# Turning five of nine input row tiles by VectorE blocks and a DRAM round trip instead of by TensorE

## The chip, the cores and the metric

The kernel runs on one core of one Trainium2 chip. The metric is the device time of one execution in microseconds (us), lower is better. The profile is of one execution; its times are in us unless marked ns.

## What is computed

One step of a decoder layer for a prompt of 1024 rows and 64 rows of new tokens (8 sequences of 8). Every row is normalised, and one wide projection feeds two attention branches and the merge gates:

```python
h = rms_norm(x, norm_g).astype(x.dtype)          # x / rms(x), times norm_g per column
z = jnp.einsum('bsd,de->bse', h, w_in)           # D_MODEL 1024, all projections side by side
...
qb = rms_norm(qb.reshape(b, s, B_HEADS, 2, HEAD_DIM), q_norm_b)
```

After that come the attention of both branches, their projections, the gates and the output projection. The change touches only the normalised input `h` and the way in which it comes to lie transposed, with the 1024 columns of the model on the partitions.

## The kernel before

The program is written by hand, one instruction stream per engine, with counted semaphores between them; each engine does its stream in the order in which it is written. Rows come in nine tiles: 0 to 7 are the prompt's (128 rows each, `NT` is 8), tile 8 is the sample's 64 rows. Weights come in blocks of 1024 x 512 (`u` is the block's number). A block is multiplied with all nine row tiles before the next one, eight chunks `k` of 128 columns each, three matmuls a chunk (`products`, L2074 to L2076), since every fp32 operand is split in a high and a low part. A row tile of a block is thus 24 matmuls. In this document "row r" of the first block is row tile r, and its "start" is its first matmul.

The first block, u = 0, is the q projection of branch B. While it runs, the row tiles are still being prepared, each in a relay over five engines:

- SyncE loads `xt` (`load_x`, L733), two buffers.
- ScalarE squares it with a running sum (`input_square`, L1292); GpSimd turns the sum into 1/rms (`input_rstd`, L1051 and L1052).
- VectorE scales the rows into `xn` (`rows_scale`, L1594).
- TensorE turns `xn` in two halves of four 128 x 128 transposes into bank 4 to 7 of PSUM (`turn_x`, L2030); of tiles 2 and up into bank 7 alone, so that a half waits until VectorE has read the one before.
- VectorE multiplies by the norm's gain on the way out of PSUM into `hn` (`input_gain`, L1603).
- ScalarE rounds to the high part (`input_hi`, L1268), GpSimd subtracts for the low part (`input_lo`, L1058), both into `hT`. TensorE's row waits for the low part (`h_lo`).

At row i of the block the engines have this work in their streams: TensorE turns tile i + 2 between its chunks; ScalarE and GpSimd do hi and lo of tile i + 3, and square and 1/rms of tile i + 4; VectorE does the gain of tile i + 3 and the scaling of tile i + 4. Between them stands what row i itself yields: a square of its result (ScalarE, L1335), the sum per head (VectorE, L1658), 1/rms (GpSimd), the scaled result `zn` (VectorE, L1673), its turning in 32 x 32 blocks (VectorE, L1679) and its store by SyncE (`store_blocks`, L768), and the splitting of one chunk of the next block's weights into high (ScalarE, L1281) and low part (VectorE, L1587). SyncE's own stream at row i (`block_io`) is `load_x(i+3)`, a weight chunk of the next block, `store_blocks` of row i - 1.

A DMA that moves 32 x 32 blocks between DRAM and the chip does so in pieces of 128 bytes. The kernel has such loads already: after the q and k projections it loads `qT` and `kT` from the blocks stored before (`load_turned`, L781).

## Time and profile before

| | |
|---|---|
| median of 3 runs | 1658.04 us |
| lowest, highest | 1654.12, 1663.19 us |
| the profiled execution | 1655.49 us, its span 1653.5 us |
| TensorE busy | 1597.9 us, 97% of the span |
| VectorE, GpSimd, ScalarE busy | 46%, 42%, 34% |
| granted TensorE clock | 0.994 of full speed over the span |

The span runs from the first to the last instruction of the engines; the profiled execution's own time is 2 us above it. The page has the share of each engine, the chain of work that ended last and the costliest groups; the trace behind it gives each instruction's start and length, what its engine waited for ahead of it, and the DMA queues. A duration in a timeline is that of one instruction or, where the row says xN, of N in a row.

### The profile page before, as it was taken

To read this page: it belongs to the slowest core of one execution; us is meant where nothing else is said; L and a number is where in the kernel's file an instruction comes from. 1 tells how busy PE (TensorE), PEld (TensorE's weight loads), DVE (VectorE), ACT (ScalarE), POOL (GpSimd) and SP (SyncE) were. 2 spreads that over 40 slices of the span, in tenths; PEclk is the share of its full clock that TensorE was granted. 3 is DMA by queue.
4 is the path that set the end of the run, shared out by engine and by line. 5 is a ranking of instruction groups with operands and counts; after the bars stand their busy time and mean duration, and the time that the engine had idled before them with its cause. 6 is when DMAs were issued, how large, how long until landed. Compare 5 with 4: busy or idle time off the path is not lost.

```text
span 1653.5 us, 37307 instructions
## 1 busy us (share of the span) xinstructions
PE 1597.9 (97%) x14616; PEld 1373.3 (83%) x14616; DVE 757.4 (46%) x1852; ACT 564.2 (34%) x1341; POOL 697.7 (42%) x958
## 2 busy tenths in 40 slices
PE   6999999999999999999999989999999899999999
PEld 5787677878899999999999877778787788888787
DVE  6632577332473332733326545344454433588411
ACT  5321477121362222712126233333343334411300
POOL 5676340466543666446666112222121121665500
PEclk9999999999999999999999999999999999999999
DMA  5358897337982369933797899889988977865593
GB/s 165 111 148 189 270 305 233 101 85 153 262 283 86 90 158 248 321 108 96 172 260 250 304 303 323 280 306 316 325 292 297 332 251 238 290 197 171 196 332 100
DMA packets 351487, 369.84 MB, mean 224 GB/s; under 512 B 164113, under 2 KB 208274, under 8 KB 351314
## 3 DMA queue, kind: packets, MB, share of 16 engines
q1 hardware_dynamic: 306354, 308.55, 61.9%
q10 hardware_dynamic: 44960, 58.92, 10.7%
q8 instruction: 117, 1.92, 0.5%
q14 instruction: 56, 0.46, 0.1%
HBM read 310.83 MB, written 143.85 MB: 275 GB/s over the span
## 4 chain that ended last, share of the span: by engine, by line
PE 84%; DVE 4%; DMA 3%; POOL 3%; issue 2%; ACT 2%; SPq 1%; ACTq 1%; POOLq 0%; DVEq 0%
PE ps L2074 13%; PE ps L2075 13%; PE ps L2076 13%; PE ps L2127 5%; PE ps L2128 5%; PE ps L2129 5%; PE ps L2230 4%; PE ps L2287 4%; PE ps L2176 4%; PE ps L2250 3%; PE ps L2348 3%; PE ps L2237 2%; PE ps L2331 2%; DMA v_in<-in_cache_a_kv 2%; PE ps L2197 2%
## 5 line engine op out<-in xcount | busy, mean ns | idle before, releaser
L1071 POOL TENSOR_TENSOR w_lo<-raw,w_hi 128x512 fp32r<-128x512 f32 x140 | 181.3, 1299 | 400.8 <-ACT w_hi L1281 399.9
L2074 PE MATMUL ps<-w_hi,hT 128*128 128x512 f32 x824 | 333.0, 404 | 2.1 <-POOL hT L1058 1.0
L2075 PE MATMUL ps<-w_lo,hT 128*128 128x512 f32 x824 | 330.1, 401 | 0.0
L2076 PE MATMUL ps<-w_hi,hT 128*128 128x512 f32 x824 | 330.1, 401 | 0.0
L2127 PE MATMUL ps<-w_hi,hT 128*128 128x256 f32 x768 | 225.3, 293 | 4.3 <-issue 3.9
L2074 PEld LDWEIGHTS ps<-w_hi,hT 128*128 128x128 f32 x824 | 206.2, 250 | 22.8 <-issue 1.4
L2076 PEld LDWEIGHTS ps<-w_hi,hT 128*128 128x128 f32 x824 | 206.2, 250 | 20.4
L2075 PEld LDWEIGHTS ps<-w_lo,hT 128*128 128x128 f32 x824 | 206.4, 250 | 19.4
L2129 PE MATMUL ps<-w_hi,hT 128*128 128x256 f32 x768 | 216.8, 282 | 1.0 <-issue 1.0
L2128 PE MATMUL ps<-w_lo,hT 128*128 128x256 f32 x768 | 217.4, 283 | 0.0
L1125 POOL TENSOR_SCALAR qz<-qT,qcol 64x128 f32<-64x128 f32 x256 | 156.0, 609 | 108.6 <-PE ps L2176 54.8
L1281 ACT ACTIVATE w_hi<-raw 128x512 fp32r<-128x512 f32 x158 | 98.7, 628 | 279.2 <-DMA raw<-in_w_in 237.0
L2127 PEld LDWEIGHTS ps<-w_hi,hT 128*128 128x128 f32 x768 | 147.3, 192 | 12.1 <-issue 11.5
L2128 PEld LDWEIGHTS ps<-w_lo,hT 128*128 128x128 f32 x768 | 147.6, 192 | 1.8 <-issue 1.8
L2129 PEld LDWEIGHTS ps<-w_hi,hT 128*128 128x128 f32 x768 | 147.2, 192 | 0.0
L1801 DVE STREAM_TRANSPOSE k_in<-k_in 128x512 f32<-128x512 f32 x224 | 138.5, 678 | 3.9 <-DMA k_in<-in_cache_a_kv 2.6
L1052 POOL TENSOR_TENSOR rs<-ss,half_pow 128x8 f32<-128x8 f32 (+3 forms) x81 | 127.0, 1568 | 6.7
L1673 DVE TENSOR_TENSOR zn<-ps,rs 128x512 f32<-128x512 f32 (+1 forms) x72 | 49.7, 691 | 145.5 <-POOL rs L1052 145.5
L1391 ACT ACTIVATE sA<-sA,st_sum 128x128 f32<-128x128 f32 (+1 forms) x192 | 86.1, 449 | 58.3 <-DVE st_sum L1767 52.4
L1335 ACT ACTIVATE ps<-ps 128x512 f32<-128x512 f32 (+1 forms) x72 | 41.8, 580 | 182.1 <-PE ps L2076 173.6
L1658 DVE TENSOR_REDUCE ss<-ps 128x8 f32<-128x512 f32 (+1 forms) x72 | 49.7, 690 | 117.0 <-ACT ps L1335 116.9
L2230 PE MATMUL ps<-kT,qz 128*128 128x128 f32 (+1 forms) x384 | 100.4, 348 | 1.0 <-issue 0.8
(229 smaller groups left out, 2758.7 us busy)
## 6 DMA issues: line engine op xcount, KB each, us to landing
out<-in_cache_a_kv SPq DMA_DIRECT2D x32, 2040.0 KB, 13.5
k_in<-in_cache_b_kv SPq DMA_DIRECT2D x128, 256.0 KB, 4.4
v_in<-in_cache_b_kv SPq DMA_DIRECT2D x128, 256.0 KB, 6.3
raw<-in_w_in SPq DMA_DIRECT2D x104, 256.0 KB, 3.4
k_in<-in_cache_a_kv SPq DMA_DIRECT2D x104, 256.0 KB, 8.1
v_in<-in_cache_a_kv ACTq DMA_DIRECT2D x96, 256.0 KB, 6.4
out<-in_cache_a_kv SPq DMA_DIRECT2D x8, 2016.0 KB, 10.3
raw<-in_w_in ACTq DMA_DIRECT2D x40, 256.0 KB, 6.8
```

The costliest lines, as they stand in the source:

```text
L1052: return pool.tensor_tensor(out, in_, half_pow[0:r, 0:heads], ALU.pow)
L1071: pool.tensor_tensor(lo, raw_of(q), hi.bitcast(F32), ALU.subtract).then_inc(lo_done, 1)
L1125: return pool.tensor_scalar(qz[rows, half, cols], qT[rows, c * SEQ + i * P:c * SEQ + (i + 1) * P], qcol[rows, (0 if G else 1):(0 if G else ...
L1281: act.activation(weights(q)[0], raw_of(q), ACT.Copy).then_inc(hi_done, 1)
L1801: dve.transpose(k_in[:, gg % NKS, j, :], k_in[:, gg % NKS, j, :]).then_inc(s_kt, 1)
L2074: pe.matmul(z, hi, wh, start=first, stop=False)
L2075: pe.matmul(z, hi, wl, start=False, stop=False)
L2076: return pe.matmul(z, lo, wh, start=False, stop=last)
L2127: pe.matmul(part, hi, wh, start=k == 0, stop=False)
L2128: pe.matmul(part, hi, wl, start=False, stop=False)
L2129: ins = pe.matmul(part, lo, wh, start=False, stop=k == KC - 1)
L2230: pe.matmul(bank(s % 4)[:, 0:W], qz[:, hh, i * P:(i + 1) * P], kT[:, k0:k0 + W], start=True, stop=True).then_inc(aq, 1)
```

## The change

Row tiles 3 to 7 (`BY_BLOCKS`) no longer go over TensorE and PSUM. VectorE multiplies the rows by 1/rms and by the gain in one instruction (the gain lies as `grow`, one copy of `norm_g` on each partition, loaded once), and turns the result in place in 32 x 32 blocks, 128 x 1024 at once. SyncE stores it to a DRAM scratch with four DMAs of 32 partitions each, in such an order that the scratch holds the tile transposed (`store_x`), waits until they have landed, and loads it back as `xT` (`load_xT`). ScalarE and GpSimd take high and low part from `xT` instead of `hn`. Tiles 0, 1, 2 and 8 go the old way.

With it the order changes: hi and lo of a turned tile t stand at row t - 2 of ScalarE's and GpSimd's streams, both halves together and at the row's end, where they stood at row t - 3 with other work between the halves. SyncE issues `load_x(i+5)` at row i behind `store_blocks`, where it issued `load_x(i+3)` ahead of it, and the weight chunks one row earlier. Semaphores used later in the program are used for the new waits too, and their later counts are raised.

```diff
@@ -212,6 +212,9 @@
...
         lamv = place("lamv", [P, 4, HD], at=at)
+        xT = place("xT", [P, 2, KC, P], at=at)
+        grow = place("grow", [P, D_MODEL], at=at)
+        assert at[0] <= work
@@ -316,6 +319,7 @@
...
         blocks_scr = [[dram(f"blocks_scr{g}{kind}", [SEQ, CW]) for kind in "qk"] for g in range(4)]
+        x_scr = [dram(f"x_scr{i}", [D_MODEL, P]) for i in range(TILES)]
@@ -406,6 +413,18 @@
...
             return turn_out[m % 2], 16 * sum(x % 18 % 9 < NT for x in range(m % 2, m + 1, 2))
+        def x_stored(i):
+            return st_in, 64 * (i - BY_BLOCKS[0] + 1)
+        def x_loaded(i):
+            return (kt_in if i % 2 else qt_in), 16 * len(range(BY_BLOCKS[0] + (i + BY_BLOCKS[0]) % 2, i + 1, 2))
+        def x_turns(i):
+            return i if i < BY_BLOCKS[0] else BY_BLOCKS[0]
@@ -573,6 +592,10 @@
...
             return half, (NT, *range(NT))[at_] if half else at_
+        def hi_lo_at(i):
+            return [t for t in (i + 2, i + 3) if (t in BY_BLOCKS) == (t == i + 2) and BY_BLOCKS[0] <= t <= NT]
@@ -746,6 +769,7 @@
...
             load_x(2)
+            sp.dma_start(grow[:, :], norm_g[0].partition_broadcast(P)).then_inc(s_const, 16)
@@ -754,6 +778,20 @@
...
                                  vec[0].rearrange("(d o) -> d o", o=1)).then_inc(s_const, 16)
+            load_x(4)
+            def store_x(i):
+                sp.wait_ge(ew_exp, i - BY_BLOCKS[0] + 1)
+                for a in range(0, P, 32):
+                    sp.dma_start(x_scr[i][:, a:a + 32].rearrange("(b r) c -> r b c", r=32),
+                                 xn[a:a + 32, i % 2, :].rearrange("p (b c) -> p b c", c=32)).then_inc(x_stored(i)[0], 16)
+            def load_xT(i):
+                sp.wait_ge(*x_stored(i))
+                if i - 2 in BY_BLOCKS:
+                    sp.wait_ge(h_lo, 2 * i - 2)
+                sp.dma_start(xT[:, i % 2, :, :], x_scr[i].rearrange("(k p) c -> p k c", p=P)).then_inc(x_loaded(i)[0], 16)
@@ -783,14 +821,18 @@
...
                 for at_, i in row_tiles(kind):
-                    if u == 0 and 4 <= i + 3 < TILES:
-                        load_x(i + 3)
...
                         constants()
-                    if at_ < KC:
-                        load_chunk(u + 1, at_)
+                    for k in ((0, 1) if at_ == 0 else (at_ + 1,)) if u == 0 else (at_,):
+                        if k < KC:
+                            load_chunk(u + 1, k)
...
                         store_blocks(G, kind, i - 1)
+                    if u == 0 and i + 5 < TILES:
+                        load_x(i + 5)
+                    if u == 0 and i + 3 in BY_BLOCKS:
+                        store_x(i + 3)
+                        load_xT(i + 3)
@@ -1056,6 +1098,7 @@
...
                     pool.tensor_tensor(hT_part(1, half, i),
+                                       xT[:, i % 2, 4 * half:4 * half + 4, :] if i in BY_BLOCKS else
@@ -1099,9 +1142,10 @@
...
                     if u == 0:
-                        input_lo(i + 3, 0)
                         input_rstd(i + 4)
-                        input_lo(i + 3, 1)
+                        for t in hi_lo_at(i):
+                            input_lo(t, 0)
+                            input_lo(t, 1)
@@ -1264,10 +1308,13 @@
...
                 if i < TILES:
-                    act.wait_ge(h_hn, 2 * i + half + 1)
-                    act.activation(hT_part(0, half, i),
-                                   hn[:, half, :].rearrange("p (k r) -> p k r", k=4)[:, :, 0:nrows(i)],
-                                   ACT.Copy).then_inc(h_hi, 1)
+                    if i in BY_BLOCKS:
+                        act.wait_ge(*x_loaded(i))
+                        part = xT[:, i % 2, 4 * half:4 * half + 4, :]
+                    else:
+                        act.wait_ge(h_hn, 2 * x_turns(i) + half + 1)
+                        part = hn[:, half, :].rearrange("p (k r) -> p k r", k=4)[:, :, 0:nrows(i)]
+                    act.activation(hT_part(0, half, i), part, ACT.Copy).then_inc(h_hi, 1)
@@ -1287,7 +1334,7 @@
...
                     if i >= 2:
-                        act.wait_ge(h_t, 2 * i - 2)
+                        act.wait_ge(*(x_stored(i - 2) if i - 2 in BY_BLOCKS else (h_t, 2 * i - 2)))
@@ -1335,8 +1382,6 @@
...
                         move(G)
-                    if u == 0:
-                        input_hi(i + 3, 0)
@@ -1344,7 +1389,9 @@
...
                         input_square(i + 4)
-                        input_hi(i + 3, 1)
+                        for t in hi_lo_at(i):
+                            input_hi(t, 0)
+                            input_hi(t, 1)
@@ -1591,12 +1638,19 @@
...
                     dve.wait_ge(h_rs, i + 1)
+                    if i in BY_BLOCKS:
+                        dve.wait_ge(s_const, 80)
+                        dve.scalar_tensor_tensor(out=xn[:, i % 2, :], in0=xt[:, i % 2, :], scalar=rs_x[:, i % 2, 0:1],
+                                                 in1=grow[:, :], op0=ALU.mult, op1=ALU.mult).then_inc(h_xn, 1)
+                        dve.wait_ge(h_xn, i + 1)
+                        dve.transpose(xn[:, i % 2, :], xn[:, i % 2, :]).then_inc(ew_exp, 1)
+                        return
...
             def input_gain(i, half):
-                if i < TILES:
-                    r, j = nrows(i), 2 * i + half
+                if i < TILES and i not in BY_BLOCKS:
+                    r, j = nrows(i), 2 * x_turns(i) + half
@@ -2021,7 +2075,7 @@
...
             def turn_x(i, half):
-                r, j = nrows(i), 2 * i + half
+                r, j = nrows(i), 2 * x_turns(i) + half
@@ -2089,7 +2143,7 @@
...
                         ins = products(bank(z_bank(n)), hi, lo, hTs[:, k, :], first_chunk[u] + k, i, k == 0, k == K - 1)
-                        if u == 0 and k in ((1, 5) if i else (4, 7)) and i + 2 < TILES:
+                        if u == 0 and k in ((1, 5) if i else (4, 7)) and i + 2 < TILES and i + 2 not in BY_BLOCKS:
```

VectorE, end of the preparation and rows 0 and 1 of the first block, before (`w_lo_72` is the first block's weight buffer, `w_lo_74` the second's, which the rows' weight splits fill):

```order
L1594 TENSOR_SCALAR xn<-xt,rs_x 128x1024 [waits h_rs]
L1603 TENSOR_TENSOR hn<-ps,gcol 128x512 [waits h_lo,h_t] x2
L1658 TENSOR_REDUCE ss<-ps 128x8 [waits sq_ready]
L1603 TENSOR_TENSOR hn<-ps,gcol 128x512 [waits h_lo,h_t]
L1673 TENSOR_TENSOR zn<-ps,rs 128x512 [waits rs_ready]
L1679 STREAM_TRANSPOSE zn<-zn 128x512 [waits zn_ready]
L1587 TENSOR_TENSOR w_lo_74<-raw,w_hi_73 128x512 [waits hi_done]
L1603 TENSOR_TENSOR hn<-ps,gcol 128x512 [waits h_lo,h_t]
L1594 TENSOR_SCALAR xn<-xt,rs_x 128x1024 [waits h_rs]
L1691 TENSOR_SCALAR qcol<-qcol 128x2 [waits s_const]
L1658 TENSOR_REDUCE ss<-ps 128x8 [waits sq_ready]
```

The same place of the changed kernel:

```order
L1643 SCALAR_TENSOR_TENSOR xn<-xt,rs_x,grow 128x1024 [waits s_const,h_rs]
L1646 STREAM_TRANSPOSE xn<-xn 128x1024 [waits h_xn]
L1657 TENSOR_TENSOR hn<-ps,gcol 128x512 [waits h_lo,h_t] x2
L1712 TENSOR_REDUCE ss<-ps 128x8 [waits sq_ready]
L1727 TENSOR_TENSOR zn<-ps,rs 128x512 [waits rs_ready]
L1733 STREAM_TRANSPOSE zn<-zn 128x512 [waits zn_ready]
L1634 TENSOR_TENSOR w_lo_74<-raw,w_hi_73 128x512 [waits hi_done]
L1643 SCALAR_TENSOR_TENSOR xn<-xt,rs_x,grow 128x1024 [waits s_const,h_rs]
L1646 STREAM_TRANSPOSE xn<-xn 128x1024 [waits h_xn]
L1745 TENSOR_SCALAR qcol<-qcol 128x2 [waits s_const]
L1712 TENSOR_REDUCE ss<-ps 128x8 [waits sq_ready]
```

The gains of the turned tiles are gone from the rows; weighting and turning stand where the scaling stood, ahead of the next row's sum and, for tile 3, ahead of the gains of tile 2.

GpSimd, rows 1 and 2 of the first block, in the changed kernel:

```order
L1093 TENSOR_SCALAR ss<-ss 128x8 [waits ss_ready]
L1094 TENSOR_TENSOR rs<-ss,half_pow 128x8 [waits pool_step]
L1093 TENSOR_SCALAR ss_x<-ss_x 128x1 [waits h_ss]
L1094 TENSOR_TENSOR rs_x<-ss_x,half_pow 128x1 [waits pool_step]
L1100 TENSOR_TENSOR hT_50<-xT,hT_49 128x4x128 [waits h_hi] x2
L1093 TENSOR_SCALAR ss<-ss 128x8 [waits ss_ready]
L1094 TENSOR_TENSOR rs<-ss,half_pow 128x8 [waits pool_step]
```

The two low halves of a tile stand together behind both 1/rms; before, the first stood between them.

SyncE, the stretch of rows 0 and 1, in the changed kernel:

```order
L756 DMA xt<-in_x_prompt 128x1024 [waits h_xn]
L787 DMA x_scr<-xn 32x32x32 [waits ew_exp]
L787 DMA x_scr<-xn 32x32x32 x3
L794 DMA xT<-x_scr 128x8x128 [waits st_in]
L763 DMA raw<-in_w_in 128x512 [waits lo_done]
L806 DMA blocks_scr0q<-zn 128x512 [waits blocks_turned]
L756 DMA xt<-in_x_prompt 128x1024 [waits h_xn]
```

Before, a row had three DMAs here (`raw`, `blocks_scr0q`, `xt`); now SyncE also issues the four stores, and stands at the load until they have landed, with the next weight chunk, the store of the row's blocks and the next `xt` behind it.

## Rows read from the trace of the kernel before

**Rows 1.** The page, chain that ended last: shares of the span by engine.

```profile
PE 84%; DVE 4%; DMA 3%; POOL 3%; issue 2%; ACT 2%; SPq 1%; ACTq 1%; POOLq 0%; DVEq 0%
```

**Rows 2.** Stretches: length, busy us of PE, PEld, DVE, ACT, POOL; clock, DMA share, GB/s.

```profile
26.54:60.91 34.37, 33.35 (x161) 25.98 (x159) 23.91 (x36) 16.75 (x32) 27.47 (x31) 1.00 0.40 124
506.00:508.00 2.00, 2.00 (x10) 2.00 (x10) 0.00 (x0) 0.00 (x0) 0.00 (x0) 1.00 0.19 17
```

**Rows 3.** Timeline, TensorE, first block: start us, us, instruction, idle before and releaser.

```profile
24.68 0.63 PE L2030 MATMUL ps<-ident,xn 128*128 128x128 f32 x4 [0.74 <-DVE hn L1603]
25.06 0.48 PE L2074 MATMUL ps<-w_hi,hT 128*128 128x512 f32 x1
26.54 0.60 PE L2030 MATMUL ps<-ident,xn 128*128 128x128 f32 x4
...
40.79 0.66 PE L2030 MATMUL ps<-ident,xn 128*128 128x128 f32 x4 [0.45 <-DVE xn L1594]
...
66.19 0.40 PE L2074 MATMUL ps<-w_hi,hT 128*128 128x512 f32 x1
...
71.79 0.40 PE L2072 MATMUL ps<-w_hi,hTs 128*128 128x512 f32 x1
```

**Rows 4.** Timeline, VectorE, row tiles 0 and 1 of the first block.

```profile
23.18 0.75 DVE L1594 TENSOR_SCALAR xn<-xt,rs_x 128x1024 f32<-128x1024 f32 x1 [0.45 <-POOL rs_x L1052]
23.85 0.68 DVE L1603 TENSOR_TENSOR hn<-ps,gcol 128x512 f32<-128x512 f32 x1
...
27.22 0.69 DVE L1658 TENSOR_REDUCE ss<-ps 128x8 f32<-128x512 f32 x1 [1.18 <-ACT ps L1335]
...
33.52 1.27 DVE L1691 TENSOR_SCALAR qcol<-qcol 128x2 f32<-128x2 f32 x1
34.70 0.68 DVE L1658 TENSOR_REDUCE ss<-ps 128x8 f32<-128x512 f32 x1
...
37.43 0.69 DVE L1673 TENSOR_TENSOR zn<-ps,rs 128x512 f32<-128x512 f32 x1 [1.46 <-POOL rs L1052]
...
38.79 0.68 DVE L1587 TENSOR_TENSOR w_lo<-raw,w_hi 128x512 fp32r<-128x512 f32 x1
```

**Rows 5.** Timeline, GpSimd, the same stretch.

```profile
33.48 1.28 POOL L1058 TENSOR_TENSOR hT<-hn,hT 128x512 fp32r<-128x512 f32 x1 [0.66 <-ACT hT L1268]
35.46 0.20 POOL L1051 TENSOR_SCALAR ss<-ss 128x8 f32<-128x8 f32 x1 [0.70 <-DVE ss L1658]
35.75 1.65 POOL L1052 TENSOR_TENSOR rs<-ss,half_pow 128x8 f32<-128x8 f32 x1
...
38.74 0.19 POOL L1051 TENSOR_SCALAR ss_x<-ss_x 128x1 f32<-128x1 f32 x1
39.01 0.86 POOL L1052 TENSOR_TENSOR rs_x<-ss_x,half_pow 128x1 f32<-128x1 f32 x1
```

**Rows 6.** Groups by line and shape, VectorE: count, busy us, mean ns, idle before.

```profile
L1801 DVE STREAM_TRANSPOSE k_in<-k_in 128x512 f32<-128x512 f32 x224 | 138.5, 678 | 3.9 <-DMA k_in<-in_cache_a_kv 2.6 <-DMA k_in<-in_cache_b_kv 1.0
L1728 DVE SCALAR_TENSOR_TENSOR sB<-sB,wB 128x1024 f32<-128x1024 f32 x4 | 5.1, 1287 | 0.1
L1915 DVE STREAM_TRANSPOSE k_new<-k_new 128x128 f32<-128x128 f32 x8 | 2.5, 311 | 0.1
```

**Rows 7.** Timeline, SyncE issuing: kT loads (1024 pieces each), statistics stores (128 pieces each).

```profile
400.85 4.26 SPq L781 DMA_DIRECT2D kT<-blocks_scr1k  x4
...
406.08 4.13 SPq L781 DMA_DIRECT2D kT<-blocks_scr1k  x4
...
503.44 4.61 SPq L875 DMA_DIRECT2D st_scr<-st  x8
```

**Rows 8.** DMA issues of three stretches: count, KB each, median us to landing.

```profile
kT<-blocks_scr1k SPq DMA_DIRECT2D x16, 128.0 KB, 4.7
...
xt<-in_x_prompt SPq DMA_DIRECT2D x8, 512.0 KB, 3.8
...
st_scr<-st SPq DMA_DIRECT2D x8, 8.0 KB, 1.5
```

More of the change, by code:

```diff
@@ L392, in build_step @@
         N_CONST = 16 * 8
+        BY_BLOCKS = range(3, NT)
+        X_TURNED, X_STORED, X_LOADED = len(BY_BLOCKS), 64 * len(BY_BLOCKS), (32, 48)
         N_COPIES = len(COPY_PARTS) * DEC_B
@@ L1137, in pad_first @@
                 pool.wait_ge(setup, 1)
-                pool.wait_ge(qt_in, 256 * (G + 1))
+                pool.wait_ge(qt_in, X_LOADED[0] + 256 * (G + 1))
                 for i in range(NT) if G else TILE_ORDER:
@@ L1518, in _ @@
                 if gg == N_GROUPS + 3:
-                    act.wait_ge(ew_exp, 1)
+                    act.wait_ge(ew_exp, X_TURNED + 1)
                     act.activation(ew[:, :, :, :], ew[:, :, :, :], ACT.Exp).then_inc(ew_exp, 1)
@@ L1689, in block_ @@
                         if i == 0:
-                            dve.wait_ge(s_const, 64)
+                            dve.wait_ge(s_const, 80)
                             dve.tensor_scalar(qcol[:, :], qcol[:, :], -(HD ** -0.5), None, ALU.mult)\
@@ L1818, in group_weights @@
             def group_weights():
-                dve.wait_ge(st_in, 48)
+                dve.wait_ge(st_in, X_STORED + 48)
                 def nm(g):
@@ L1830, in group_shares @@
             def group_shares():
-                dve.wait_ge(ew_exp, 2)
+                dve.wait_ge(ew_exp, X_TURNED + 2)
                 for g in range(3):
@@ L1921, in _ @@
                         dve.wait_ge(o_out, stored(3))
-                        dve.wait_ge(s_const, 64 + 16 * 6)
+                        dve.wait_ge(s_const, 80 + 16 * 6)
                     for i in range(4):
@@ L2260, in _ @@
                 pe.wait_ge(t_moved, G + 1)
-                pe.wait_ge(kt_in, 256 * (G + 1))
+                pe.wait_ge(kt_in, X_LOADED[1] + 256 * (G + 1))
                 attention_a(G) if G else attention_b()
```

## The prediction

> **What bounds the kernel now.** I read the page first, then the stretch of the first block, then each engine's timeline in it. TensorE is busy for 97% of the span (the table), and 84% of the span is its work on the chain that ended last [rows 1]: time taken from or put into its stream moves the end, nearly one for one, and after the first block its stream is unchanged. So the question is when TensorE leaves the first block. Tile 3's first turn starts at 26.54, tile 8's at 60.91 (the stretch in [rows 2]); between them lie five rows of 24 matmuls and the ten turning groups of tiles 3 to 7. TensorE is busy 33.35 of these 34.37 us, though VectorE only 23.91 and GpSimd 27.47. Row 7 has no turns and takes 71.79 - 66.19 = 5.60 us [rows 3]; five such rows are 28.0. The rest, 34.37 - 28.0 = 6.4 us, is what turning costs: ten groups at some 0.54, and waits for `xn` of 0.45 at the first half of tile 5 [rows 3] (one like it at tile 4). Every other engine has room only because a row takes 6.7 us.
>
> **What the change removes.** Forty transposes in ten groups, with their waits: at most 6.4 us, if each row's low part is there in time. The ten gains on VectorE (0.68 each, as that of tile 2 [rows 4]) go too; they are simply missing from the lists below.
>
> **What it adds on VectorE.** Weighting reads two SBUF operands of 128 x 1024; the same instruction and shape takes 1.29 us elsewhere [rows 6]. The bounds are 0.75, the plain scaling it replaces [rows 4], and 1.29 plus the low half of 1.28 that it may have to wait for (see the low halves, below). I take 1.29. The turning of 128 x 1024 has no row: 128 columns take 0.31 and 512 take 0.68 [rows 6], so on the line through them 1.17; twice 0.68 is the upper bound, 1.36. I take 1.2. The pair is 2.5 us where 0.75 stood.
>
> **The preparation.** The pair of tile 3 stands ahead of the gains of tile 2: the first of them starts at 23.85, right behind the scaling of 23.18 [rows 4], and will start 1.8 us later. TensorE's second turn of tile 2 waits for it (the idle 0.74 at 24.68), and row 1 follows that turn, at 25.06 [rows 3]. So row 1 starts at 26.9 and the sum of row 0 on VectorE, at 27.22 before, at 29.0. This 1.8 is on the path and nothing covers it.
>
> **One row of VectorE's stream.** From a row's sum to its `zn` 2.7 us (34.70 to 37.43; GpSimd's part of it is the wait for 35.46, then 35.75 plus 1.65 [rows 4, 5]), from `zn` over its own turning to the weight split 1.4 (37.43 to 38.79), the split 0.65, weighting 1.3, turning 1.2: 7.2 us, against 5.6 that TensorE needs. Before, the same cycle had two gains (one within the wait for GpSimd) and the scaling, some 6.2, and fitted the row of 6.7. For tile 4: 29.0 + 7.2 = 36.2, plus the small scaling of `qcol`, so row 1's sum starts at 36.5 though its matmuls are done at 32.5.
>
> **How the two low halves fit in.** `qcol` is 128 x 2 and yet took 1.27 us at 33.52, until 34.8, which is when GpSimd's low half of 33.48 ended (1.28 long) [rows 4, 5]. A VectorE scaling in SBUF stood still until GpSimd's subtraction was over. I assume the same for the weight split and the weighting, which read two operands from SBUF, and none for the turning. In the changed order a row on GpSimd, counted from the sum's start, is: 1/rms of the row done at 2.7, that of the next tile (38.74 to 39.87, 1.1 [rows 5]) at 3.8, first low half to 5.1. The split, due at 4.1, waits until 5.1 and ends at 5.75; the second low half goes to 7.05; the weighting to 8.3, the turning to 9.5. So the cycle is **9.5 us**, not 7.2.
>
> The Trainium skill, SBUF — State Buffer, "Who interferes with whom", says that a VectorE instruction with two SBUF inputs and a GpSimd instruction that reads SBUF exclude each other for their whole length. By that rule the weighting waits too, which the trace shows only for the plain scaling; without it, the sum would be that of the first rival.
>
> **When rows start.** Row t needs its first low half, at 5.1 after the sum of row t - 2. Row 3: 36.5 + 5.1 = 41.6 (before: 40.79 less the wait of 0.45 and six matmuls of 0.23, 38.9). Rows 4, 5, 6 follow at 9.5 each: 51.1, 60.6, 70.1. Tile 7 is turned at 36.5 + 3 x 9.5 = 65.0.
>
> **The round trip.** Four stores in pieces of 128 bytes. The nearest rows are loads of such pieces: four kT loads are issued in 4.26 us, and the next four follow 5.2 later with a weight chunk between [rows 7], so 4.3 us of DMA for four. A last landing takes between 1.5 (stores of 64-byte pieces) and 4.7 (kT loads that queue) [rows 8]; the last store is issued some 3.2 behind the first, so all have landed after 4.7 to 7.9. I take 6.2. `xT` is as large as an `xt` load, 3.8 us [rows 8], 3.9 with the wait. On SyncE the next weight chunk, `store_blocks` and `xt` queue behind this wait; with four issues of some 0.4 a tile costs it 6.2 + 1.7 = 7.9, under 9.5, so tiles 4 to 6 are there in time (tile 5 turned at 46.0, back at 56.2, its high part wanted around 59). Tile 3 has 11 us more. For tile 7 nothing is ahead: 65.0 + 6.2 + 3.9 = 75.1, high part 0.65 as before, low half 1.3: row 7 starts at **77.1** instead of 66.19. With the ends of the landing 76.9 (then GpSimd's own queue is last: the sum of row 5 at 72.8, plus 2.7, plus 1.3) to 78.8.
>
> `grow` is one more load of 512 KB, issued around 8 us and wanted at 24.5: I cost it at nothing; at worst it holds the weight chunks behind it by its own 3.8 [rows 8]. `load_x(5)` goes ahead of `store_blocks`; the waits of 0.45 that its lateness causes are in the 6.4 already.
>
> **The sum.** 77.1 - 66.2 = +10.9: the 6.4 are saved, and 17.3 of waits come in, 1.8 ahead of row 1 and 15.5 ahead of rows 3 to 7. Behind it, VectorE still has the sums of rows 6 and 7 to catch up on when TensorE wants the sample's `zn`; I add 0.5. In all +11.4 on the profiled execution's 1655.5, which is 2.5 under the median of 1658.0 and inside its spread of 1654 to 1663; on the median it gives 1669.4, some 0.7% slower.
>
> **Rivals.**
> (a) The lock spares the weighting and the split. Then VectorE's cycle is 7.2 and SyncE's 7.9 is the longer: stores start at 36.4, 44.3, 52.2, 60.1, tile 7 is back at 70.2 and row 7 starts at 72.2: +6.0, with the 0.5 behind it 1664.5. For it: four instructions of the weighting's kind and shape average 1.287 [rows 6], so none of them was held up. Against it: `qcol`.
> (b) Stores of 128-byte pieces are slow. If the four take 8.6 of DMA instead of 4.3, a tile costs SyncE 10.5 + 1.7 = 12.2: stores at 36.4, 48.6, 60.8, 73.0, row 7 at 89.4: +23.2, with the 0.5 1681.7. Against it: eight stores of 64-byte pieces, 128 each, are issued in 4.61 us, one every 0.58 [rows 7], at a DMA share of 0.19 [rows 2], so 0.19 x 16 x 0.58 / 128 = 14 ns for a piece and engine; kT's are 4.3 x 16 / 4096 = 17 ns. The Trainium skill, DMA: Bandwidth & Descriptors, "Specifications", states that below 512 bytes an engine reads, modifies and writes; no row here shows that for stores, and it is this rival's mechanism.
> (c) The other side: the relay runs ahead and TensorE finds every low part ready. All 6.4 are kept: 1651.6, 0.4% under the median. It turns on one thing, VectorE's cycle with the pair in it: at 5.6 or below it holds, and the lists give 7.2 without any lock. The pair would have to shrink from 2.5 to 0.9. For it speaks only that VectorE was idle for a third of the stretch; but that idle time is the wait for GpSimd inside the 2.7.
> That the change does not do what it says is ruled out: of TensorE's stream exactly ten groups of four are gone, and nothing else.
>
> **Chances.** The forecast 0.58 (1666 to 1674 with its bounds), (a) 0.18, (b) 0.12, (c) 0.07, anything else 0.05. The range from 1660 to 1680 holds the forecast, (a), and the lower half of (b). A measurement of this kernel tells some 0.5%, 8.3 us, from no change. Slower by more than that: the forecast but for its lower edge, (b): 0.66. Within: (a), (c) and that edge: 0.31. Faster 0.03.
>
> **What would show it.** Row 1 starts near 26.9 and TensorE waits for tile 2's gain. TensorE idles ahead of rows 3 to 7, released by GpSimd's `hT`, 2 to 5 us each. Weight splits and weightings of over 1.5 us beside low halves of 1.3: the lock; at 0.65 and 1.3, (a). Stores landing over 8 us after the first: (b), and SyncE late for `xT`. From row 7 on, everything is displaced by the same amount. The forecast is wrong if rows follow at under 7 us, or if a later stage, which waits on nothing of the first block, gives time back.

## The result, and the profile after

| | before | after |
|---|---|---|
| median (executions beside each other) | 1656.08 us (4) | 1678.47 us (4), 1673.78 to 1685.07 |
| the profiled execution, its span | 1655.49, 1653.5 us | 1675.98, 1674.0 us |
| granted TensorE clock over the span | 0.994 | 0.987 |

The ratio is 1.0118, 95% interval 1.0083 to 1.0154: slower by 1.2%, about 19.5 us (the two medians are 22.4 apart). The forecast was 1669.4 us, 0.7% slower, in a range from 1660 to 1680. So sign and range held, and the size came out 8 us short. Of the 19 executions of before that ran beside only_7 and before_scratch, one was in a slower state (2524 us at a granted clock of 0.561); it is left out of every ratio, and the median of the other 18 is 1656.7 us.

In what follows, the displacement at a place is the start of one and the same instruction in another trace less its start in the first trace of before. Here it is at four places for all traces: the turning of the sample's `zn` on TensorE (82.16 us in before, early in block 1), and ScalarE instructions that begin at 179, 865 and 1602 us in before. The experiments are told below. Each line is one execution; after and again, and before and before_again, are twice the same kernel and show how far two executions of one kernel differ.

| trace | 82 | 179 | 865 | 1602 |
|---|---|---|---|---|
| after | +13.0 | +17.1 | +18.4 | +20.5 |
| again | +12.8 | +14.8 | +15.4 | +22.4 |
| no_trip | +9.2 | +12.9 | +13.4 | +22.4 |
| no_weight | +11.7 | +14.7 | +15.5 | +20.1 |
| short_lows | +11.9 | +17.1 | +17.7 | +19.0 |
| both_off | +6.7 | +8.4 | +9.0 | +13.6 |
| busy_te | +13.0 | +13.6 | +13.9 | +20.6 |
| pieces_512 | +10.2 | +11.8 | +12.7 | +19.7 |
| late_pair | +13.9 | +16.8 | +18.0 | +15.2 |
| only_7 | +1.9 | +2.6 | +2.7 | -1.1 |
| before_again | 0.0 | +0.2 | +0.1 | +0.8 |
| before_scratch | +0.6 | +0.5 | +0.7 | +0.4 |
| before_delayed | +13.4 | +14.0 | +14.4 | +14.3 |

So 13 of the 20 us are lost in the first block, and the rest behind it, where not one instruction of TensorE's stream was changed. The first block first.

TensorE's timeline there, the rows with an idle time of note (start us, us, instruction, in brackets the idle time before and who ended it). In before, rows 3 to 7 came without such waits [rows 3]:

```profile
26.85 0.63 PE L2084 MATMUL ps<-ident,xn 128*128 128x128 f32 x4 [2.53 <-DVE hn L1657]
...
41.72 0.47 PE L2128 MATMUL ps<-w_hi,hT 128*128 128x512 f32 x1 [1.52 <-POOL hT L1100]
...
50.53 0.47 PE L2128 MATMUL ps<-w_hi,hT 128*128 128x512 f32 x1 [2.97 <-POOL hT L1100]
...
59.64 0.47 PE L2128 MATMUL ps<-w_hi,hT 128*128 128x512 f32 x1 [1.73 <-POOL hT L1100]
...
70.12 0.76 PE L2128 MATMUL ps<-w_hi,hT 128*128 128x512 f32 x1 [4.63 <-POOL hT L1100]
```

Rows 3 to 6 wait for the low half; row 7 began at 79.20 without a wait, against 66.19 in before [rows 3], and that difference of 13.0 is the whole displacement of block 1.

VectorE's timeline for two of the rows, which answers to [rows 4]:

```profile
36.73 0.68 DVE L1712 TENSOR_REDUCE ss<-ps 128x8 f32<-128x512 f32 x1
39.47 0.69 DVE L1727 TENSOR_TENSOR zn<-ps,rs 128x512 f32<-128x512 f32 x1 [2.06 <-POOL rs L1094]
40.20 0.71 DVE L1733 STREAM_TRANSPOSE zn<-zn 128x512 f32<-128x512 f32 x1
40.83 1.29 DVE L1634 TENSOR_TENSOR w_lo<-raw,w_hi 128x512 fp32r<-128x512 f32 x1
42.05 2.32 DVE L1643 SCALAR_TENSOR_TENSOR xn<-xt,rs_x,grow 128x1024 f32<-128x1024 f32 x1
44.40 1.25 DVE L1646 STREAM_TRANSPOSE xn<-xn 128x1024 f32<-128x1024 f32 x1
45.57 0.65 DVE L1712 TENSOR_REDUCE ss<-ps 128x8 f32<-128x512 f32 x1
...
54.36 0.65 DVE L1712 TENSOR_REDUCE ss<-ps 128x8 f32<-128x512 f32 x1
```

The sums follow at 8.84 and 8.79 us: this is VectorE's cycle, and it is idle in it only for the wait of 2.06 for GpSimd's 1/rms. The weight split takes 1.29 instead of 0.65 and the weighting 2.32, where it takes 1.28 and 1.27 with no low half beside it (at 23.56 and 34.22). GpSimd at the same time:

```profile
39.80 0.55 POOL L1094 TENSOR_TENSOR rs_x<-ss_x,half_pow 128x1 f32<-128x1 f32 x1
40.31 2.98 POOL L1100 TENSOR_TENSOR hT<-xT,hT 128x512 fp32r<-128x512 f32 x2
```

SyncE's queue, where `x_scr` and `xT` are new:

```profile
45.67 4.75 SPq L787 DMA_DIRECT2D x_scr<-xn  x4
52.96 0.38 SPq L794 DMA_DIRECT2D xT<-x_scr  x1
53.39 0.58 SPq L763 DMA_DIRECT2D raw<-in_w_in  x1
54.01 0.43 SPq L806 DMA_DIRECT2D blocks_scr0q<-zn  x1
54.49 0.47 SPq L756 DMA_DIRECT2D xt<-in_x_sample  x1
55.00 5.01 SPq L787 DMA_DIRECT2D x_scr<-xn  x4
62.68 0.38 SPq L794 DMA_DIRECT2D xT<-x_scr  x1
...
64.30 5.14 SPq L787 DMA_DIRECT2D x_scr<-xn  x4
72.05 0.38 SPq L794 DMA_DIRECT2D xT<-x_scr  x1
```

From the first store of a tile to the load that waits for its landing 7.3, 7.7 and 7.75 us, then 2.0 and 1.6 for the load, the two or three other issues and what they wait for: 9.3 a tile, twice. Tile 5's turning ended at 45.65 and its store went at once; tile 6's ended at 54.44 (53.19 + 1.25) and its store went at 55.00, tile 7's at 63.56 and 64.30. SyncE is already behind VectorE there. Over such a tile the DMA engines are busy for 0.80 and 0.83 of the time, against 0.40 over the whole stretch in before [rows 2] (stretches: length, busy us and counts of PE, PEld, DVE, ACT, POOL, then clock, DMA share, GB/s):

```profile
45.67:55.00 9.33, 6.36 (x22) 4.72 (x21) 7.21 (x7) 3.33 (x6) 5.51 (x6) 0.82 0.80 189
55.00:64.30 9.30, 7.57 (x33) 5.82 (x32) 7.01 (x7) 3.33 (x6) 5.63 (x7) 1.00 0.83 193
```

### The profile page after: what moved, and what is told of

Same layout as the page of the kernel before. It is cut to its first block, busy times and chain, and to the rows that moved or that the text cites. A ratio compares the mean times of both kernels' runs of the same rounds, so it can differ in the third digit from the quotient of the medians.

```text
span 1674.0 us, 37236 instructions
## 1 busy us (share of the span) xinstructions
PE 1600.2 (96%) x14576; PEld 1372.4 (82%) x14576; DVE 763.9 (46%) x1847; ACT 564.1 (34%) x1341; POOL 697.4 (42%) x958
## 4 chain that ended last, share of the span: by engine, by line
PE 81%; DMA 6%; DVE 4%; POOL 2%; issue 2%; ACT 2%; SPq 2%; ACTq 0%; POOLq 0%; DVEq 0%
PE ps L2128 13%; PE ps L2130 12%; PE ps L2129 12%; PE ps L2181 5%; PE ps L2182 5%; PE ps L2183 5%; PE ps L2284 4%; PE ps L2341 4%; PE ps L2230 3%; PE ps L2304 3%; PE ps L2402 3%; DMA v_in<-in_cache_a_kv 2%; PE ps L2291 2%; PE ps L2385 2%; PE ps L2251 2%
## 5 line engine op out<-in xcount | busy, mean ns | idle before, releaser
L2128 PE MATMUL ps<-w_hi,hT 128*128 128x512 f32 x824 | 335.6, 407 | 13.0 <-POOL hT L1100 11.9
L2128 PEld LDWEIGHTS ps<-w_hi,hT 128*128 128x128 f32 x824 | 207.9, 252 | 36.6 <-issue 13.9
L1093 POOL TENSOR_SCALAR ss<-ss 128x8 f32<-128x8 f32 (+3 forms) x81 | 16.0, 197 | 214.0 <-DVE ss L1712 194.7
## 6 DMA issues: line engine op xcount, KB each, us to landing
out<-in_cache_a_kv SPq DMA_DIRECT2D x8, 2016.0 KB, 10.1
```

The lines of the kernel that those rows point to most:

```text
L2128: pe.matmul(z, hi, wh, start=first, stop=False)
```

## The experiments

My theory: VectorE's cycle with the pair in it, stretched by GpSimd's low halves, sets the pace. Its rivals: the round trip on SyncE sets it; TensorE's clock, which fell in this stretch, costs the rest; and, for what is lost behind block 0, scatter of the loads, the delay as such, or the memory's layout.

**again.** No edit.

> The changed kernel once more, unaltered. In its first trace the displacement against before was +13.0 us when block 1 began, +17.0 by 165 us and +20.5 at the end. If what came behind block 0 (a late weight chunk of block 2, waits for loads in the decode part) follows from the change, the second trace shows the same steps at the same places: +13, +17, +20. If it is the scatter of the DMA engines, the +13 of block 0 comes again and the rest does not, so that the profiled run lies near 1655.5 + 13 = 1668.5. Median: 1669 to 1678.

Median 1675.93 us of 4 (1670.88 to 1680.36), ratio 1.0115 (1.0078 to 1.0152). The displacements are +12.8, +14.8, +15.4 and +22.4. The loss of block 0 comes again to 0.2 us. What lies behind it comes again too, though in other portions, so it is neither a fixed sequence of steps nor mere bad luck of one execution.

**no_trip: no waiting for the stores.**

```diff
+                if i - 1 in BY_BLOCKS:
+                    sp.wait_ge(*x_stored(i - 1))
...
-                sp.wait_ge(*x_stored(i))
                 if i - 2 in BY_BLOCKS:
                     sp.wait_ge(h_lo, 2 * i - 2)
-                sp.dma_start(xT[...], x_scr[i].rearrange("(k p) c -> p k c", p=P))
+                sp.dma_start(xT[...], x_p[0, i * P:(i + 1) * P, :].rearrange("p (k c) -> p k c", c=P))
```

> Stores of tiles 3 to 7 as they are, but the load of xT no longer waits for them: it reads the same 512 KB from the input x in the same pieces (so the hidden rows of these tiles are not normalised, weighted or turned; the computed values of all that follows are others, the work is the same). If VectorE's cycle of 8.8 to 9.1 us sets the pace (my theory), rows 3 to 6 still follow at 8.5 to 9 us and only what lies behind the last turning becomes shorter, by 2 to 3 us: block 1 begins 10 to 11 us later than in before. If the round trip on SyncE sets it (stores' landing, then xT), a tile costs SyncE 5 us, rows follow at the 7.2 of VectorE or less, and block 1 begins 3 to 6 us later than in before.

The first two lines of the edit stand ahead of a tile's stores: they wait until the tile before has landed. TensorE's rows in this trace:

```profile
49.56 0.47 PE L2129 MATMUL ps<-w_hi,hT 128*128 128x512 f32 x1 [2.96 <-POOL hT L1101]
58.34 0.48 PE L2129 MATMUL ps<-w_hi,hT 128*128 128x512 f32 x1 [1.42 <-POOL hT L1101]
67.11 0.47 PE L2129 MATMUL ps<-w_hi,hT 128*128 128x512 f32 x1 [2.94 <-POOL hT L1101]
```

Block 1 +9.2. Rows 3 to 6 start at 40.77, 49.56, 58.34 and 67.11, 8.8 apart, and the stores too (35.85, 44.71, 53.49, 62.28), each right behind its turning, so that the added wait holds none of them. So VectorE's cycle alone gives this pace, as the theory says, and the trip adds what lies behind the last turning. Of the 3.8 gained, 0.9 is not the trip's: tile 3 is weighted at 22.63 instead of 23.56 in this execution, ahead of the first instruction that the edit changes. That leaves 2.9, within the 2 to 3 I expected.

**no_weight: the weighting left out.**

```diff
-                        dve.scalar_tensor_tensor(out=xn[:, i % 2, :], in0=xt[:, i % 2, :], ... in1=grow[:, :], ...)
-                        dve.wait_ge(h_xn, i + 1)
-                        dve.transpose(xn[:, i % 2, :], xn[:, i % 2, :]).then_inc(ew_exp, 1)
+                        dve.transpose(xn[:, i % 2, :], xt[:, i % 2, :]).then_inc(h_xn, 1)
+                        dve.wait_ge(h_xn, i + 1)
+                        dve.sem_inc(ew_exp, 1)
```

> The weighting of tiles 3 to 7 is left out: VectorE turns xt directly into xn (so these rows are not normalised; later values are others). If VectorE's cycle sets the pace, it falls by the weighting's 2.3 us to 6.6, SyncE's 7.7 a tile becomes the longest, rows follow at 7.5 to 8, and block 1 begins 6 to 8 us later than in before instead of 13. If SyncE's round trip sets the pace already, nothing but the start moves, by 1.3 us: +11 to +12.

Block 1 +11.7: only 1.3 us better, what I had set down for the rival. VectorE's cycle fell to 6.3 and 6.7 us and then it waited for TensorE, so it is no longer the limit, but stores start at 34.60, 44.14, 54.20 and 63.54, that is 9.5, 10.1 and 9.3 apart, slower than VectorE's cycle had been; the last three tiles had been turned at 40.97, 47.02 and 55.56, so that it was SyncE that came late. So two limits of almost the same height lie on each other: VectorE's 8.8 to 9.1 and SyncE's 9.3 to 10.1, and taking away the one uncovers the other.

**short_lows: GpSimd's low halves shortened.**

```diff
+                    if i in BY_BLOCKS:
+                        pool.tensor_tensor(hT_part(1, half, i)[:, 0:1], xT[:, i % 2, 4 * half:4 * half + 1, :],
+                                           hT_part(0, half, i)[:, 0:1].bitcast(F32), ALU.subtract).then_inc(h_lo, 1)
+                        return
...
+            for k in (1, 5):
+                link(pool.memset(hT[1][:, k:k + 3, BY_BLOCKS[0] * P:SEQ].bitcast(F32), 0.0))
```

> GpSimd's low halves of tiles 3 to 7 cover one chunk of four (128 columns in place of 512); the other low parts of these rows are zero, set once at the start (the sums of block 0 and all later ones miss these low parts). If the stretched weighting (2.3 us) and split (1.3 us) come from these subtractions, they return to 1.3 and 0.65 us, VectorE's cycle to 7.0 to 7.3, SyncE's 7.7 is the longest, and block 1 begins 7 to 9 us later than in before. If something else stretches them (the stores' reads of SBUF, or the loads' writes), weighting stays above 2 us and block 1 begins 11 to 13 us later.

VectorE's timeline, the same row of the program as above and the next sums:

```profile
40.83 0.90 DVE L1639 TENSOR_TENSOR w_lo<-raw,w_hi 128x512 fp32r<-128x512 f32 x1
41.65 1.27 DVE L1648 SCALAR_TENSOR_TENSOR xn<-xt,rs_x,grow 128x1024 f32<-128x1024 f32 x1
...
44.12 0.65 DVE L1717 TENSOR_REDUCE ss<-ps 128x8 f32<-128x512 f32 x1
...
51.45 0.65 DVE L1717 TENSOR_REDUCE ss<-ps 128x8 f32<-128x512 f32 x1
```

The weighting is back at 1.27, the cycle at 7.33: the low halves were what stretched it. The gain does not arrive. SyncE's stores start at 45.00, 55.26 and 64.71, up to 10.3 apart, for tiles turned at 44.21, 51.54 and 58.65, and block 1 is at +11.9. The stretch costs 1.5 us per row on VectorE and, with the trip as it is, 1.1 us in all.

**both_off: no_trip and short_lows together.**

> The edits of no_trip and short_lows together: xT's load waits for no store and reads the input x, GpSimd's low halves of tiles 3 to 7 cover one chunk of four (what is computed from these rows is other than the reference's). Alone, the first brought block 1 forward from +13.0 to +9.2 us, the second to +11.9 (VectorE's cycle fell to 7.35, then the round trip, 9.3 to 10 us a tile on SyncE, held the rows). If the two are limits of nearly the same height, of which each hides the other, together they give more than the sum of 3.8 and 1.1: rows 3 to 7 follow at 7.3, and block 1 begins 3 to 5 us later than in before. If the gains only add, it begins 8 us later.

SyncE's queue:

```profile
50.92 6.35 SPq L789 DMA_DIRECT2D x_scr<-xn  x4
...
58.80 0.72 SPq L807 DMA_DIRECT2D blocks_scr0q<-zn  x1
...
60.54 4.54 SPq L789 DMA_DIRECT2D x_scr<-xn  x4
```

Block 1 +6.7. Here too the preparation was early, by 0.7 (tile 3's stores at 25.47 instead of 26.16). Without that the two together give 5.6 us, and apart 2.9 and 1.1: each hid part of the other. It is less than I hoped for (+3 to +5), because stores start at 36.12, 43.55 and 50.92, 7.4 apart, but the last at 60.54, though tile 7 was turned at 58.21. Two things hold it. With everything closer together the four stores of 50.92 took 6.35 us to issue, and the DMA engines were busy for 0.98 of the time from 43.55 to 50.92 and 0.89 from there to 60.54, which points to them as the next limit. And from 59.52, when the queue was through with the store ahead, to 60.54 it waited for the landing of tile 6's stores, 1.0 us that the experiment itself adds.

**pieces_512: larger pieces in the stores.**

```diff
-                    sp.dma_start(x_scr[i][:, a:a + 32].rearrange("(b r) c -> r b c", r=32),
-                                 xn[a:a + 32, i % 2, :].rearrange("p (b c) -> p b c", c=32)).then_inc(...)
+                    sp.dma_start(x_scr[i].rearrange("(p k) c -> p k c", k=KC)[a:a + 32],
+                                 xn[a:a + 32, i % 2, :].rearrange("p (k c) -> p k c", c=P)).then_inc(...)
```

> The four stores of tiles 3 to 7 write the same 512 KB in pieces of 512 bytes instead of 128 (1024 pieces instead of 4096; the scratch then holds the rows in another order, so what is computed from them is other than the reference's). Everything waits as in the changed kernel. If the number of pieces is what the round trip costs, the four are issued in under 3 us instead of 5, the last has landed within 4 to 5 us of the first instead of 7.5, SyncE's tile falls from 9.3 to 6 to 7.5 us, VectorE's cycle of 8.8 alone is left, and block 1 begins 9 to 10.5 us later than in before, as without the round trip. If the bytes or the latency are what it costs, the stores still take 7 us or more and block 1 begins 12 to 13 us later.

SyncE's queue:

```profile
54.48 1.72 SPq L787 DMA_DIRECT2D x_scr<-xn  x4
58.41 0.38 SPq L794 DMA_DIRECT2D xT<-x_scr  x1
...
63.28 1.72 SPq L787 DMA_DIRECT2D x_scr<-xn  x4
66.76 0.38 SPq L794 DMA_DIRECT2D xT<-x_scr  x1
```

The same bytes in a quarter of the pieces: issued in 1.72 us instead of 5.0, landed 3.9 and 3.5 us after the first instead of 7.7 (5.0 instead of 7.3 for tile 5). Stores follow at 8.8, as VectorE sets it, and block 1 is at +10.2. So the 128-byte pieces cost 2.3 to 4.3 us a tile and 2.8 us of the 13, nearly the 2.9 that no_trip gains by dropping the whole wait. The Trainium skill, DMA: Bandwidth & Descriptors, "Why small descriptors are slow (HBM only)", gives as reasons a fixed overhead per packet and the descriptor's own bytes; this trace agrees that the same bytes cost more in smaller pieces, and cannot tell those reasons from the read-modify-write of its section "Specifications".

**late_pair: tile 3's pair behind tile 2's gains.**

```diff
-            rows_scale(3)
             input_gain(2, 0)
             input_gain(2, 1)
+            rows_scale(3)
```

> Tile 3 is weighted and turned behind the two gains of tile 2 on VectorE instead of ahead of them; nothing else is changed. TensorE's second turn of tile 2 starts near 25 us instead of 26.85 and row 1 with it. If the pair's place costs what I put it at (1.8 us that every later row inherits through the sum of row 0), sums and row starts come 1 to 1.8 us earlier and block 1 begins 11.2 to 12 us later than in before. If VectorE's stream takes the same 2.5 us a little later, the sum of row 0 stays at 29 and nothing is gained: 12.7 to 13.

The first half of the expectation came true: TensorE's wait of 2.53 is gone, the sum of row 0 starts at 28.13 instead of 29.39, that of row 1 at 35.28 instead of 36.73. And yet block 1 is at +13.9, later than in the changed kernel. SyncE's queue shows why:

```profile
28.23 3.50 SPq L787 DMA_DIRECT2D x_scr<-xn  x4
34.67 0.38 SPq L794 DMA_DIRECT2D xT<-x_scr  x1
...
36.67 5.66 SPq L787 DMA_DIRECT2D x_scr<-xn  x4
44.86 0.38 SPq L794 DMA_DIRECT2D xT<-x_scr  x1
```

Tile 3's store, now 2.1 us later, leaves SyncE no pause before tile 4's, which had been turned at 35.33 and goes out at 36.67; its `xT` is asked for at 44.86 instead of 42.75. From there on SyncE is the limit: stores at 36.67, 46.86, 56.86, 65.98. Neither of the two cases in the expectation happened. The place of the pair, which I had put down as a cost of 1.8 us, is a gain of 0.9 in this one trace (two traces of the changed kernel differ by 0.2 there).

**busy_te: TensorE never idle.**

```diff
+                        if u == 0 and k == 0:
+                            filler((0, 0, 0, 6, 11, 7, 16, 7, 0)[i])
                         if u == 0 and k % 4 == 0:
                             pe.wait_ge(h_lo, 2 * i + k // 4 + 1)
```

> The changed kernel with TensorE kept busy where it waited: 9 matmuls of 128x512 into a bank that nothing reads ahead of the second turn of tile 2, and 6, 11, 7, 16, 7 ahead of rows 3 to 7. If the clock falls because TensorE idled, it stays at 2.4 GHz, row 6 takes 5.6 us instead of 9.1, row 7 then waits for GpSimd's low half (done at 78.4 in the changed kernel) and block 1 begins 12.0 to 12.5 us later than in before instead of 13.0: the fall costs at most 1 us at the end, since rows wait anyhow. If the clock has another cause, rows 1, 4 and 6 stay slow and block 1 begins 13 to 16 us later. Ratio to before 1.010 to 1.013 either way.

Nine more fillers stand ahead of tile 2's second turn. Row 6 in both kernels (stretches as above, first of the changed kernel, then of this one):

```profile
70.12:79.20 9.08, 9.08 (x32) 6.64 (x33) 2.73 (x5) 1.88 (x4) 5.00 (x5) 0.72 0.67 197
```

```profile
70.04:79.10 9.06, 8.68 (x40) 6.23 (x40) 2.89 (x6) 2.05 (x5) 4.38 (x5) 1.00 0.74 207
```

With fillers in the place of the waits the granted clock is 1.00 in each stretch from 26 to 90 us. Without them it is 0.72 in row 6, whose first matmuls came 0.43 us apart (the lower level, 1.2 GHz) and the later ones 0.233 (2.4 GHz), after 4.63 us of idling. So the idling is what lowers the clock. It buys nothing: row 7 now waits for GpSimd until 79.10, since tile 7's stores took 8.4 us to land here (64.19 to 72.60) instead of 7.75; block 1 is at +13.0, and the ratio is 1.0112 (1.0080 to 1.0144). In the changed kernel the first low half of tile 7 was done at 78.4 (77.13 + 1.27), TensorE with row 6 at 79.20, so the slow clock cost 0.8 us at most.

**only_7: one tile alone.**

```diff
-        BY_BLOCKS = range(3, NT)
+        BY_BLOCKS = range(7, NT)
```

(and hi and lo of a tile t of 3 to 6 at row t - 3 again, as in before).

> Only tile 7 goes by 32x32 blocks and the scratch; tiles 3 to 6 are turned on TensorE as in before, with the changed kernel's earlier loads of x. It saves two groups of four turns, 1.1 us, and one wait for a late x. Its pair falls in VectorE's row 3, turned near 52.5 us; with a round trip of 12 us from turning to low half (7.5 stores, 3.9 load, 2 on ScalarE and GpSimd less what overlaps) row 7 is ready at 65 to 66 where it is wanted at 65. If the loss of the change is one of rate (VectorE's cycle, SyncE's tile, added up over five tiles), block 1 begins 0 to 1.5 us earlier than in before. If it is one of latency that a single tile pays as well, block 1 begins 3 us later or more. Ratio to before 0.998 to 1.002 in the first case.

Median 1657.79 us of 10 beside 1656.7 of before, ratio 1.0014 (0.9989 to 1.0039); block 1 +1.9, between my two cases. TensorE's waits, then SyncE's trip:

```profile
61.68 0.46 PE L2092 MATMUL ps<-ident,xn 64*128 64x64 f32 x4 [1.52 <-DVE xn L1656]
...
68.02 0.47 PE L2136 MATMUL ps<-w_hi,hT 128*128 128x512 f32 x1 [0.93 <-POOL hT L1100]
```

```profile
56.36 2.54 SPq L787 DMA_DIRECT2D x_scr<-xn  x4
61.66 0.39 SPq L794 DMA_DIRECT2D xT<-x_scr  x1
```

The 11.66 us from store to row 7 (56.36 to 68.02) are almost what I had taken, 12. The pair came later than the 52.5 of my expectation: VectorE reaches tile 7's weighting at 53.79 and ends its turning at 56.34. TensorE waits 1.52 for the sample tile's `xn`, which VectorE scales behind that pair, and 0.93 for the low half. One tile loses 1.9 us, five lose 13.0: the latency costs something once, the larger part is rate.

**before_again, before_delayed, before_scratch: what is lost behind block 0.** The first has no edit; the second has 56 matmuls ahead of row 7, into a bank that nothing reads; the third declares `x_scr` and leaves it unused.

```diff
+                        if u == 0 and k == 0 and i == 7:
+                            for _ in range(56):
+                                pe.matmul(bank(4), hT[0][:, 0, 0:P], weights(0)[0], start=True, stop=True)
```

```diff
+        x_scr = [dram(f"x_scr{i}", [D_MODEL, P]) for i in range(TILES)]
         os_scr = dram("os_scr", [2, DEC_B, ROW_C, P])
```

> The kernel before, unaltered, for a second trace. Behind block 0 every trace of the changed kernel and its variants loses another 1.4 to 4 us up to 165 us (TensorE waits for the last weight chunk of block 2) and 1 to 9 us in the decode part (waits for v_in). If these are consequences of the change, this trace lies within 0.3 us of the first one of before at 165 us and within 2 us at the end. If the loads scatter by themselves, it too is displaced, by 1 to 4 us at 165 us and up to 5 in the decode part.

> The kernel before, with 56 more matmuls of 128x512 on TensorE ahead of row 7 of block 0 (into a bank that nothing reads), 13.0 us at 0.233: the displacement of the changed kernel without its change. If a displacement alone costs only itself, the time is before's plus 13.0 us, ratio 1.0079. If what is lost behind block 0 comes from the delay as such (DMA traffic that does not wait for TensorE then falls elsewhere), the ratio is 1.010 to 1.013, as that of the changed kernel. By the theory that it comes from the new order of loads on SyncE or from the stores, it is 1.008.

> The kernel before with the nine scratch tensors x_scr declared and never used, so that the scratch tensors behind them lie 4.5 MB further on in memory as in the changed kernel. Seven traces with the change lose 1.3 to 9 us between 865 us and the end against the first trace of before, two of before's kind only 0 to 0.7. If the memory's layout is the cause, this one loses 2 to 6 us there and its ratio is 1.001 to 1.004. If it is not, the trace lies within 1 us and the ratio is 0.999 to 1.001.

before_again lies within 0.2 us until 865 us and 0.8 at the end: before's trace is reproducible. before_scratch is at +0.4 at the end, its ratio 0.9980 (0.9953 to 1.0006): the layout is not the cause. before_delayed starts block 1 at +13.4, the place where the changed kernel starts it, and ends at +14.3, with a ratio of 1.0095 (1.0066 to 1.0124), against 1.0118 and 1.0115 for the changed kernel. So a delay of 13 us costs 14 to 16, not 20. Its interval and those of the changed kernel overlap, so the times alone do not settle that there is more; the traces speak for it, since between 82 and 179 us the nine traces with tiles 3 to 7 by blocks lose 0.6 to 5.2 more, on average 2.7, and the four others -0.2 to 0.7.

One place of that loss can be named. When block 2 begins, TensorE waits for the low part of its last weight chunk, 3.39 us in the changed kernel:

```profile
145.42 0.50 PE L2126 MATMUL ps<-w_hi,hTs 128*128 128x512 f32 x1 [3.39 <-POOL w_lo L1114]
```

The stretches of that wait and behind it (columns as above):

```profile
142.00:146.30 4.30, 0.91 (x5) 0.75 (x5) 1.00 (x2) 1.89 (x4) 1.27 (x1) 1.00 0.76 186
146.30:150.30 4.00, 4.00 (x13) 3.10 (x11) 1.94 (x4) 0.48 (x1) 2.65 (x3) 0.58 0.00 0
```

In the traces of before, before_again and before_delayed that wait is 0.9, 1.1 and 1.5 us; in again 2.9, in busy_te 1.4, and in the seven others with five tiles by blocks 2.3 to 3.4. The load of that chunk was issued at 138.10 and landed by 143.39, 5.3 us, against 3.8 in before and 3.7 in before_delayed. After the wait of 3.39 the clock fell once more (0.58 over 4.0 us). There nothing hides it, and it costs 1.6 us. Why a load takes 1.5 us longer nearly 70 us after the last store of the change, through the same queue in the same order, no run here shows. From 865 us on the kernels with five tiles by blocks lose between -2.8 and +9.0 us, but executions of before alone spread from 1648.6 to 1666.2 us, so that part is not settled either.

## Why the prediction held in sign and fell short in size

The range of 1660 to 1680 held, the forecast's own bounds of 1666 to 1674 did not, and that the range held is in part luck. At row 7 the forecast was 2.1 us short (+13.0 instead of +10.9), the 0.5 that it added did not exist, and 6.5 us came from behind the first block, where it had nothing.

- **TensorE's saving** is there: ten groups of turns are gone, row 7 still takes 5.6 us.
- **Weighting 1.29, turning 1.2** (estimates): 1.28 and 1.25. Row 1's start "at 26.9": 27.2.
- **The lock.** The forecast took the stretching by GpSimd's low halves as real on the strength of one row, `qcol`, and it was: short_lows gives 1.27 back. The Trainium skill, SBUF — State Buffer, "Who interferes with whom", says that the two exclude each other for their whole length; the trace agrees: the weighting of 42.05 ends at 44.37, 1.1 us after GpSimd's second low half (43.29), which is nearly its own length. The size was a little off, 8.8 to 9.1 us a row instead of 9.5: the low halves started 3.6 us after the sum, not 3.8, and the weighting ended 7.6 after it, not 8.3.
- **Row starts** of 41.6, 51.1, 60.6 and 70.1 were measured at 41.72, 50.53, 59.64 and 70.12. The last one agrees for another reason than the forecast's: by then SyncE was late, and tile 6's high part had to wait for `xT` until 67.76, so that the row no longer hung on VectorE's cycle.
- **SyncE's 7.9 a tile, under 9.5** is the term that failed. It was 9.3, at least as long as VectorE's 8.8 to 9.1. I had taken 6.2 for stores and landing from rows of other stretches [rows 7, 8]; with weight chunk, `xt`, `store_blocks` and `xT` in the same queues it was 7.3 to 7.75, inside my bounds of 4.7 to 7.9 but at their far end, and the load waits behind it for 4.4 instead of 3.9. VectorE turned tile 7 at 63.56, 1.4 sooner than the 65.0 of the forecast; SyncE then took it up 0.7 late, and stores and load took 1.55 and 0.5 longer, so that errors partly cancelled. Tile 7 thus had its first low half at 78.4 instead of 77.1, inside the forecast's ends of 76.9 to 78.8. That row 7 began at 79.20, outside them, is the fallen clock, up to 0.8 us, a term that the sum did not have.
- **The 1.8 us ahead of row 1**, "on the path and nothing covers it", is refuted by late_pair. The delay was real, but the path led through SyncE, which gained from the pair's early place.
- **+0.5 at the sample's `zn`**: the wait is 0.88 us, in before 0.87. It does not exist.
- **"From row 7 on, everything is displaced by the same amount"** is false. It was +13.0 at 82 us and +17.1 at 179; in the repeat +12.8 and +14.8. This, with what follows in the last stages, is the larger part of the 8 us that the forecast fell short; before_delayed shows that 0.9 to 2.3 of them come with any such delay (+14.3 in its trace, 15.7 in its time, for 13.4), the rest stays open.
- **Rival (a)**, no lock and +6.0, falls twice: the lock is there, and without it (short_lows) the round trip holds the rows at +11.9. **Rival (b)** had the right mechanism, small pieces (2.3 to 4.3 us of a tile's 7.3 to 7.75 by pieces_512), but not the size that it needed: 7.7 for a tile's stores, not 10.5, and +13.0, not +23.2. **Rival (c)** asked for a cycle of 5.6 on VectorE; the shortest with tiles 3 to 7 by blocks is 6.3, between the first two sums of no_weight, which leaves half of the pair out.

## What to carry to other kernels

Where work is moved from the bounding engine into a relay over others, add up each station's whole period, its queue's issues and waits included, and compare all of them with the one period that is to be kept. Here TensorE wanted a row each 5.6 us, VectorE needed 8.8 and SyncE 9.3, and repairing either alone was worth 1 to 3 of the 13 us. A DMA that turns data by being cut into 128-byte pieces has to be costed by its pieces, in queues as full as they will be then.

## What the runs showed of the hardware

- The same 512 KB to DRAM were issued and landed in 7.3 to 7.75 us in 4096 pieces (changed kernel, tiles 5 to 7) and in 3.5 to 5.0 us in 1024 (pieces_512, the same tiles), in the same queue with the same neighbours. For tiles 3 and 4, with less traffic beside them, it was 5.6 and 6.0 against 4.1 and 4.1.
- A VectorE instruction with two SBUF operands beside GpSimd's subtractions took 2.3 us instead of 1.28 (the weighting), a split 1.29 instead of 0.65, and GpSimd's pair of subtractions 2.98 instead of 2.54. VectorE's 32x32 turning of 128x1024 took 1.25 in the changed kernel, with no low half beside it, and 1.23 in no_weight (at 39.74), within a pair of low halves (38.00 to 40.98).
- TensorE's granted clock fell to 0.50 behind the waits of 2.53, 2.97 and 4.63 us in the first block of the changed kernel (0.72 over the whole of row 6) and to 0.58 over 4.0 us behind the later one of 3.39; it stayed at 1.00 behind those of 1.52 and 1.73, and when matmuls stood in the waits' place (busy_te). Where a later wait absorbed the slow stretch, it cost nothing at the end of the block.
